# Differential attention: each head's two sample steps placed among its prompt steps, with the weight splitting on them

## The chip, the cores and the metric

The kernel runs on one core of a Trainium2 chip. The metric is the device time of one launch in microseconds. Work is shared by five engines, each with its own in-order queue: TensorE (PE, matrix products and transposes), VectorE (DVE), ScalarE (ACT), GpSimd (POOL) and SyncE (SP); here the last two only start transfers in the stage that is changed. Engines wait for each other on semaphores.

## The reference

One layer of a hybrid encoder, for a prompt of 1024 tokens and a sample of 256, with shared weights. Its differential attention, 4 heads with two maps of depth 64 each and values of width 128:

```
s = einsum('qd,kd->qk', q_c, k_c) * DA_DK ** -0.5 - slope[h] * |pos_q - pos_k|     # c = 0, 1
p_c = softmax(s)
attn = p_0 - lam * p_1
o = attn @ v                                                  # swept over blocks of 128 queries
o_da = head_rms(o, g_da) * (1.0 - lam_init)
mix = concatenate([o_hg, o_da]);  x = x + mix @ w_out         # w_out: 1024 x 1024
```

The prompt and the sample attend only to their own tokens. Before it comes the input projection and the other group of heads (hgrn), behind it the output projection, a cross attention and a mixture of 32 experts.

## The kernel before

The program is a sequence of stages with a barrier between them: `front`, `hgrn`, `diff_attention`, `mix_out`, `project`, `cross_and_experts`. Matrix products are made from operands split into a rounded high part and a low part (three products for one). So a weight must be split before use: ACT rounds it, DVE subtracts.

`diff_attention` works in steps, one for a block of 128 queries (number t) of one head (h): 4 heads with 8 blocks of the prompt, then 4 heads with 2 blocks of the sample, 40 in all. A prompt step has 1024 keys, a sample step 256. The parts of step n and the lines where they stand:

- `scores` (PE, L1309): both score maps, into `score_ps`, which exists once; waits until DVE has read the scores of step n - 1.
- `find_least` (DVE, L1225): adds the distance bias, writes `score` and its least value, for both maps. The trace shows it as CUSTOM_DVE_ANT_0 with a short read of the accumulator behind it.
- `exps` (ACT, L1270): the two exponentials with their sums.
- `attention` (DVE, L1233, L1235, L1238): reciprocal, share, and the difference of the two maps.
- `transposes` (PE, L1319), `copy_attention` (ACT, L1278 and the small L1279), `output` (PE, L1331).
- `head_rstd` (ACT, L1286, L1288, L1290) and `head_norm` (DVE, L1246), after which POOL stores the tile (L1202).

Each engine runs the same outer loop, and in iteration `at` it does its parts of several steps: a part with lead k does step `at + k`. The leads and the order in the iteration are

```
skewed((2, attention), (0, head_norm), (4, find_least), (0, ride))    # DVE
skewed((3, exps), (1, head_rstd), (2, copy_attention), (0, ride))     # ACT
skewed((4, scores), (1, output), (2, transposes))                     # PE
```

`ride` is the weight split: during this stage `w_out` is split in eight pieces of 128 rows (`WeightSplit`). SP loads a piece (L174) into one of two buffers, ACT rounds it (L179, `w_w_high<-da_split_raw`) at the end of its iteration, and DVE subtracts (L184, `w_w_low<-da_split_raw,w_w_high`) at the end of its own, after a wait for ACT's rounding. The table `riders` says in which iterations.

Of the kernel before, what the change touches and what calls it, by code (L numbers as in the profile page):

```python
# [37 lines left out]
P = 128  # L38
D = 1024
KC = D // P  # L40
SEQ_P, SEQ_S, N_MEM = 1024, 256, 256
# [4 lines left out]
HEADS = 4  # L46
# [1087 lines left out]
def diff_attention(nc, tag, dq_t, dk_t, dv_rows, g_da, lam, ident, eps, mix_out, split):  # L1134
# [3 lines left out]

    slopes = [2.0 ** (-8.0 * (h + 1) / HEADS) for h in range(HEADS)]
    width = 2 * SEQ_P - P  # L1140
    steps = [(first, seq, h, t) for first, seq in ((0, SEQ_P), (SEQ_P, SEQ_S)) for h in range(HEADS)
             for t in range(seq // P)]
    N = len(steps)
    riders = {N - KC + r: r for r in range(KC)}
    with Mem(nc, tag) as m:
        keys = m.sb("keys", [P, HEADS, T])
        query = m.sb("query", [P, HEADS, T])
# [26 lines left out]
        def skewed(*parts):  # L1174
            for at in range(-max(lead for lead, _ in parts), N):
                for lead, part in parts:
                    if 0 <= at + lead < N:
                        part(at + lead)

        with nc.Block() as block:  # L1180
            @block.sync
            def _(sp):
                for h in range(HEADS):
                    rows = slice(h * P, (h + 1) * P)
                    sp.dma_start(query[:, h], dq_t[rows, :]).then_inc(qk_in[h], 16)
                    sp.dma_start(keys[:, h], dk_t[rows, :]).then_inc(qk_in[h], 16)
                    if h == 0:
                        sp.dma_start(v[:], dv_rows.rearrange("(t p) c -> p t c", p=P)).then_inc(v_in, 16)
                        with nc.allow_non_contiguous_dma(reason="one row for all partitions"):
                            sp.dma_start(gain[:], g_da.rearrange("(a n) -> a n", a=1).to_broadcast([P, P])  # L1190
                                         ).then_inc(gain_in, 16)
                for r in range(KC):
                    rider.load(sp, r // 2, r % 2)
# [12 lines left out]
            @block.vector  # L1206
            def _(dve):
                rider.start(dve)
                dve.tensor_scalar(minus_lam[:], lam[:], -1.0, None, ALU.mult)
                dve.wait_ge(where_done, 1)  # L1210
                dve.scalar_tensor_tensor(where, where, -1.0, where, ALU.mult, ALU.max).then_inc(distance_done, 1)
                dve.wait_ge(gain_in, 16)
                dve.tensor_scalar(gain[:], gain[:], 1.0 - LAM_INIT, None, ALU.mult)
                dve.drain()

                def find_least(n):
                    first, seq, h, t = steps[n]
                    u, col = n % 2, SEQ_P - P - t * P
                    dve.wait_ge(scores_ready, n + 1)
                    if n < HEADS * SEQ_P // P:  # L1220
                        dve.wait_ge(bias_done, h + 1)
                    if n >= 2:
                        dve.wait_ge(prob_done, n - 1)
                    for c in range(2):
                        done = dve.tensor_tensor_reduce(out=score[:, u, c, 0:seq], in0=score_ps[:, c, 0:seq],  # L1225
                                                        in1=bias[:, h, col:col + seq], scale=1.0, scalar=3.0e38,
                                                        op0=ALU.add, op1=ALU.min, accum_out=least[:, u, c:c + 1])
                    done.then_inc(score_read, 1)

                def attention(n):  # L1230
                    u, seq = n % 2, steps[n][1]
                    dve.wait_ge(prob_done, n + 1)
                    dve.reciprocal(share[:, u:u + 1], total[:, n % 4, 1:2])  # L1233
                    dve.drain()
                    dve.scalar_tensor_tensor(share[:, u:u + 1], total[:, n % 4, 0:1], minus_lam[:, 0:1], share[:, u:u + 1],  # L1235
                                             ALU.mult, ALU.mult)
                    dve.drain()
                    dve.scalar_tensor_tensor(prob[:, u, 0, 0:seq], prob[:, u, 1, 0:seq], share[:, u:u + 1],  # L1238
                                             prob[:, u, 0, 0:seq], ALU.mult, ALU.add).then_inc(attn_done, 1)

                def head_norm(n):
                    u = n % 2
                    dve.wait_ge(rstd_done, n + 1)
                    if n >= 2:
                        dve.wait_ge(stored[u], 16 * (n // 2))
                    dve.scalar_tensor_tensor(o[:, u], o_ps[:, u, 0:P], rstd[:, u:u + 1], gain[:], ALU.mult,  # L1246
                                             ALU.mult).then_inc(o_done, 1)

                def ride(n):
                    if n in riders:  # L1250
                        rider.subtract(dve, riders[n] // 2, riders[n] % 2)

                skewed((2, attention), (0, head_norm), (4, find_least), (0, ride))

            @block.scalar
# [1135 lines left out]
def encoder(nc, x_prompt, x_sample, mem_prompt, mem_sample, g_mix, w_in, hg_lb, g_hg, lam_q1, lam_k1, lam_q2,  # L2391
# [16 lines left out]
    with Mem(nc, "kept") as kept:  # L2408
# [17 lines left out]
        with Mem(nc, "w") as m:  # L2426
            w_at = m.next_address()
            w_high, w_low = m.sb("w_high", [P, KC, D], F32R), m.sb("w_low", [P, KC, D], F32R)
            diff_attention(nc, "da", dq_t, dk_t, dv_rows, g_da[0], lam, ident, eps, mix, (w_out[0], w_high, w_low))
            with Mem(nc, "cq") as m2:  # L2430
                high, low = m2.sb("high", [P, KC, T], F32R), m2.sb("low", [P, KC, T], F32R)
                mix_out(nc, "mix_out", o_fwd, o_bwd, g_rows, mix, x_rows, g_hg[0], w_high, w_low, ident, eps, x1,
                        g_ca[0], high, low)
                project(nc, "proj_q", w_cq[0], D, high, low, TOKEN_GROUPS, q_t, split=(w_co[0], w_high, w_low))
            cross_and_experts(nc, "cross", q_t, kv_t, x1, w_high, w_low, w_at, ident, eps, x2, g_ffn[0], w_rg[0],
                              b_rg[0], w_re[0], b_re[0], h3, w_gate[0].rearrange("e k n -> (e k) n"),
                              w_up[0].rearrange("e k n -> (e k) n"), w_down[0].rearrange("e k n -> (e k) n"), y_rows,
                              g_final, [(y_prompt[0], NT_P), (y_sample[0], NT - NT_P)])
# [28 lines left out]
```

## Time and profile before

| | |
|---|---|
| median of 3 runs | 2228.51 us (2226.96 to 2229.07) |
| the profiled execution | 2223.16 us, of which the span from first to last instruction is 2221.7 us |
| busy share of the span | PE 89%, DVE 62%, ACT 52%, POOL 12% |
| differential attention | from some 735 to 952 us of the span |
| its prompt steps | a step every 4.77 us |
| weight split in it | 8 pieces; ACT 1047 ns and DVE 1225 ns each |
| mean granted PE clock | 0.942 of 2.4 GHz |

Times of a row are microseconds from the start of the span; PEclk is the granted share of 2.4 GHz, so 0.50 is 1.2 GHz. The profile's own chain of what ended last covers only the late stages; for this stage the timeline tells who waits for whom.

### The profile page before, as it was taken

The page shows a single profiled execution, that of the slowest core. Times are in us where ns is not written, and L with a number is a line of the kernel's source. Part 1 is how long each engine was busy: PE and PEld are TensorE (multiplying, and loading weights), DVE is VectorE, ACT ScalarE, POOL GpSimd, SP SyncE. Part 2 cuts the span into 40 slices and gives each one's busy share as a digit, 9 for nine tenths or more (in the row PEclk, how much of TensorE's full clock was granted, in tenths as well). Part 3 has the DMA queues.
Part 4 walks back from the last instruction along what each step waited for, and adds up shares of the span by engine and source line. Part 5 has one row for each costly group of instructions (what it writes and reads, how often), then busy time and mean ns, then how long its engine had stood idle before and what let it go on. Part 6 is the DMA issues. An engine that isn't in the chain of part 4 may idle for free. (4 is left out here: it accounts for less than half of the span.)

```text
span 2221.7 us, 31173 instructions
## 1 busy us (share of the span) xinstructions
PE 1977.8 (89%) x11108; PEld 1639.3 (74%) x11108; DVE 1375.1 (62%) x1841; ACT 1149.1 (52%) x1587; POOL 265.4 (12%) x304
## 2 busy tenths in 40 slices
PE   6999999969999699749989499996999999999990
PEld 5888888857888477438778388885888888888870
DVE  4222231029998488646511035546999999999986
ACT  4334432116665488713222133222888888888873
POOL 0000000020000011100000000000122223232210
PEclk9999999989999899769989799996999999999995
DMA  5223422135553400144233423134899999999987
GB/s 170 102 93 136 144 97 105 47 114 168 164 176 106 179 15 15 63 149 161 95 109 113 149 86 114 61 149 158 324 382 383 383 378 383 377 380 391 378 319 317
DMA packets 162983, 423.97 MB, mean 191 GB/s; under 512 B 18880, under 2 KB 84544, under 8 KB 136768
## 3 DMA queue, kind: packets, MB, share of 16 engines
q1 hardware_dynamic: 137424, 342.37, 43.1%
q0 software_dynamic: 25456, 80.24, 9.4%
q8 instruction: 63, 1.03, 0.2%
q14 instruction: 40, 0.33, 0.0%
HBM read 354.92 MB, written 82.31 MB: 197 GB/s over the span
## 5 line engine op out<-in xcount | busy, mean ns | idle before, releaser
L113 PE MATMUL cross_ot_ps<-w_w_high,cross_o_high 128*128 128x512 f32 x544 | 220.5, 405 | 3.1 <-DVE cross_o_low L2126 2.4
L115 PE MATMUL cross_ot_ps<-w_w_high,cross_o_low 128*128 128x512 f32 x544 | 213.8, 393 | 0.0
L113 PE MATMUL front_acc<-in_high,front_w_high 128*128 128x512 f32 (+1 forms) x480 | 170.3, 355 | 0.0
L114 PE MATMUL front_acc<-in_low,front_w_high 128*128 128x512 f32 (+1 forms) x480 | 170.0, 354 | 0.0
L115 PE MATMUL front_acc<-in_high,front_w_low 128*128 128x512 f32 (+1 forms) x480 | 169.8, 354 | 0.0
L2093 DVE TENSOR_TENSOR cross_low_up<-cross_raw_up,w_w_high 128x2048 fp32r<-128x2048 f32 x68 | 152.8, 2288 | 12.0 <-ACT w_w_high L1904 12.0
L2093 DVE TENSOR_TENSOR cross_low_down<-cross_raw_down,w_w_low 128x2048 fp32r<-128x2048 f32 x68 | 152.7, 2287 | 1.7 <-ACT w_w_low L1904 1.7
L2093 DVE TENSOR_TENSOR w_w_low<-cross_raw_gate,w_w_high 128x2048 fp32r<-128x2048 f32 x68 | 152.2, 2279 | 0.0
L1904 ACT ACTIVATE w_w_high<-cross_raw_up 128x2048 fp32r<-128x2048 f32 x68 | 126.2, 1907 | 0.0
L1904 ACT ACTIVATE w_w_low<-cross_raw_down 128x2048 fp32r<-128x2048 f32 x68 | 126.2, 1907 | 0.0
L1904 ACT ACTIVATE w_w_high<-cross_raw_gate 128x2048 fp32r<-128x2048 f32 x68 | 126.1, 1902 | 0.0
L113 PEld LDWEIGHTS cross_ot_ps<-w_w_high,cross_o_high 128*128 128x128 f32 x544 | 103.2, 190 | 30.1 <-DVE w_w_low L2093 7.2
L115 PEld LDWEIGHTS cross_ot_ps<-w_w_high,cross_o_low 128*128 128x128 f32 x544 | 103.0, 189 | 22.2
L113 PE MATMUL cross_out_ps<-w_w_low,cross_ht 128*128 128x512 f32 x272 | 109.5, 403 | 5.5 <-DVE cross_low_down L2093 5.5
L114 PE MATMUL cross_ot_ps<-w_w_low,cross_o_high 128*128 128x512 f32 x272 | 107.6, 395 | 0.0
L115 PE MATMUL cross_out_ps<-w_w_low,cross_ht 128*128 128x512 f32 x272 | 107.0, 393 | 0.0
L114 PE MATMUL cross_out_ps<-cross_low_down,cross_ht 128*128 128x512 f32 x272 | 106.8, 393 | 0.0
L114 PE MATMUL cross_ot_ps<-cross_low_up,cross_o_high 128*128 128x512 f32 x272 | 106.0, 390 | 0.0
L113 PE MATMUL front_acc<-front_w_high,in_high 128*128 128x512 f32 x240 | 95.2, 397 | 6.0 <-DVE front_w_low L565 6.0
L113 PEld LDWEIGHTS front_acc<-in_high,front_w_high 128*128 128x128 f32 x480 | 90.8, 189 | 12.9
L114 PEld LDWEIGHTS front_acc<-in_low,front_w_high 128*128 128x128 f32 x480 | 90.8, 189 | 12.6
L115 PEld LDWEIGHTS front_acc<-in_high,front_w_low 128*128 128x128 f32 x480 | 90.7, 189 | 12.6
(361 smaller groups left out, 4889.3 us busy)
## 6 DMA issues: line engine op xcount, KB each, us to landing
cross_raw_gate<-in_w_gate_dram SPq DMA_DIRECT2D x68, 1024.0 KB, 7.0
cross_raw_down<-in_w_down_dram SPq DMA_DIRECT2D x68, 1024.0 KB, 7.9
cross_raw_up<-in_w_up_dram SPq DMA_DIRECT2D x68, 1024.0 KB, 9.4
front_raw<-in_w_in_dram SPq DMA_DIRECT2D x32, 512.0 KB, 4.4
hgrn_raw<-in_w_ckv_dram SPq DMA_DIRECT2D x16, 512.0 KB, 6.7
cross_y_kept<-y_rows SPq DMA_DIRECT2D x16, 512.0 KB, 9.4
k_t<-front_staged POOLq DMA_DIRECT2D x8, 640.0 KB, 3.3
lf_t<-front_staged_lf POOLq DMA_DIRECT2D x8, 640.0 KB, 4.6
```

Of the source, the lines that this page charges most:

```text
L113: pe.matmul(out, lhs[0], rhs[0], start=first, stop=False)
L114: pe.matmul(out, lhs[0], rhs[1], start=False, stop=False)
L115: return pe.matmul(out, lhs[1], rhs[0], start=False, stop=last)
L1904: act.activation(w_high[s][:, cols], raw[s][:, cols], ACT.Copy).then_inc(w_high_done[s], 1)
L2093: dve.tensor_tensor(w_low[s][:, cols], raw[s][:, cols], w_high[s][:, cols].bitcast(F32), ALU.subtract).then_inc(w_low_done[s], 1)
```

## The change

The order of the steps is changed. In each head, the two sample steps are put among the eight prompt steps, at places 2 and 7 of ten, so that a sample step is every fifth step (n = 2, 7, 12, ..., 37). The eight pieces of the weight split, which rode on the last eight steps, ride on the sample steps again, which are now spread over the stage. DVE's wait for the bias is made in every step. Sizes, leads, buffers and the number of instructions of each kind are the same; names of lines shift by one (DVE's L1225 is L1226 after).

```diff
-    steps = [(first, seq, h, t) for first, seq in ((0, SEQ_P), (SEQ_P, SEQ_S)) for h in range(HEADS)
-             for t in range(seq // P)]
+    order = [(0, t) for t in range(SEQ_P // P)]
+    for t in range(SEQ_S // P):
+        order.insert(2 + 5 * t, (SEQ_P, t))
+    steps = [(first, SEQ_S if first else SEQ_P, h, t) for h in range(HEADS) for first, t in order]
     N = len(steps)
-    riders = {N - KC + r: r for r in range(KC)}
+    riders = {n: r for r, n in enumerate(n for n in range(N) if steps[n][0])}
...
                     dve.wait_ge(scores_ready, n + 1)
-                    if n < HEADS * SEQ_P // P:
-                        dve.wait_ge(bias_done, h + 1)
+                    dve.wait_ge(bias_done, h + 1)
```

On DVE, at the end of iteration 2 and through iteration 3, early in the stage (`da_` are this stage's tiles, `w_w_high` and `w_w_low` the parts of the weight). Before:

```order
L1225 ISA da_least 128x1
L1233 RECIPROCAL da_share<-da_total 128x1
L1235 SCALAR_TENSOR_TENSOR da_share<-da_total,da_minus_lam,da_share 128x1
L1238 SCALAR_TENSOR_TENSOR da_prob<-da_prob,da_share 128x1024
L1246 SCALAR_TENSOR_TENSOR da_o<-da_o_ps,da_rstd,da_gain 128x128
L1225 ISA da_score,da_least<-da_score_ps,da_bias 128x1024
L1225 ISA da_least 128x1
```

And now:

```order
L1226 ISA da_least 128x1
L184 TENSOR_TENSOR w_w_low<-da_split_raw,w_w_high 128x1024
L1234 RECIPROCAL da_share<-da_total 128x1
L1236 SCALAR_TENSOR_TENSOR da_share<-da_total,da_minus_lam,da_share 128x1
L1239 SCALAR_TENSOR_TENSOR da_prob<-da_prob,da_share 128x1024
L1247 SCALAR_TENSOR_TENSOR da_o<-da_o_ps,da_rstd,da_gain 128x128
L1226 ISA da_score,da_least<-da_score_ps,da_bias 128x256
L1226 ISA da_least 128x1
```

The subtraction of the weight stands between one step's find_least and the attention of a prompt step (128x1024), and the find_least behind that attention is a sample step's (128x256). The same pattern returns every five steps; in all of them but the last it is a prompt step's attention that stands behind the subtraction.

On ACT, at the same iterations (`da_attn_t` is the copy of the transposed attention). Before:

```order
L1278 ACTIVATE da_attn_t<-da_attn_ps 128x1024
L1279 ACTIVATE da_eps_t<-da_total 128x1
L1270 ACTIVATE da_prob,da_total<-da_score,da_least 128x1024 x2
L1286 ACTIVATE da_sq,da_ss<-da_o_ps 128x128
L1288 ACTIVATE da_rstd<-da_ss,da_eps_t 128x1
L1290 ACTIVATE da_rstd<-da_rstd 128x1
```

And now:

```order
L1279 ACTIVATE da_attn_t<-da_attn_ps 128x1024
L1280 ACTIVATE da_eps_t<-da_total 128x1
L179 ACTIVATE w_w_high<-da_split_raw 128x1024
L1271 ACTIVATE da_prob,da_total<-da_score,da_least 128x1024 x2
L1287 ACTIVATE da_sq,da_ss<-da_o_ps 128x128
L1289 ACTIVATE da_rstd<-da_ss,da_eps_t 128x1
```

The rounding of the weight stands behind the copy of a prompt step's transposed attention and ahead of the exponentials of another prompt step.

## Rows read from the trace of the kernel before

**Rows 1.** Busy time by stretch: PE, PEld, DVE, ACT, POOL, PEclk, DMA share, GB/s.
```profile
800.00:850.00 50.00, 50.00 (x338) 35.39 (x338) 44.31 (x85) 42.97 (x106) 5.41 (x10) 1.00 0.04 14
...
935.00:950.00 15.00, 3.83 (x12) 2.44 (x12) 7.15 (x12) 6.62 (x17) 2.16 (x4) 0.50 0.36 122
```

**Rows 2.** Timeline, one prompt step: start, us, engine, line, operation, [idle before <-releaser].
```profile
846.18 2.05 PE L1331 MATMUL da_o_ps<-da_v,da_attn_t 128*128 128x128 f32 x16
...
846.30 1.23 DVE L1225 CUSTOM_DVE_ANT_0 da_score<-da_score_ps,da_bias 128x1024 f32<-128x1024 f32 x1 [0.40 <-PE da_score_ps L1309]
...
848.07 1.04 PE L1319 MATMUL da_attn_ps<-kept_ident,da_prob 128*128 128x128 f32 x8
...
848.27 0.28 ACT L1286 ACTIVATE da_sq<-da_o_ps 128x128 f32<-128x128 f32 x1 [0.50 <-PE da_o_ps L1331]
...
848.59 0.16 DVE L1233 RECIPROCAL da_share<-da_total 128x1 f32<-128x1 f32 x1
...
849.03 1.99 PE L1309 MATMUL da_score_ps<-da_keys,da_query 64*128 64x512 f32 x8
...
849.18 1.01 ACT L1278 ACTIVATE da_attn_t<-da_attn_ps 128x1024 f32<-128x1024 f32 x1
...
850.17 1.14 ACT L1270 ACTIVATE da_prob<-da_score,da_least 128x1024 f32<-128x1024 f32 x1
850.32 0.34 DVE L1246 SCALAR_TENSOR_TENSOR da_o<-da_o_ps,da_rstd,da_gain 128x128 f32<-128x128 f32 x1
...
850.95 1.27 PE L1331 MATMUL da_o_ps<-da_v,da_attn_t 128*128 128x128 f32 x9
850.96 0.54 POOL L1202 DMA_DIRECT2D mix<-da_o  x1 [4.23 <-DVE da_o L1246]
851.07 1.22 DVE L1225 CUSTOM_DVE_ANT_0 da_score<-da_score_ps,da_bias 128x1024 f32<-128x1024 f32 x1 [0.41 <-PE da_score_ps L1309]
```

**Rows 3.** Timeline, a sample step with the first split.
```profile
916.61 0.41 DVE L1225 CUSTOM_DVE_ANT_0 da_score<-da_score_ps,da_bias 128x256 f32<-128x256 f32 x1
...
916.95 0.42 DVE L1225 CUSTOM_DVE_ANT_0 da_score<-da_score_ps,da_bias 128x256 f32<-128x256 f32 x1
...
918.76 1.05 ACT L179 ACTIVATE w_w_high<-da_split_raw 128x1024 fp32r<-128x1024 f32 x1
...
919.91 1.23 DVE L184 TENSOR_TENSOR w_w_low<-da_split_raw,w_w_high 128x1024 fp32r<-128x1024 f32 x1 [2.54 <-ACT w_w_high L179]
...
921.05 0.16 DVE L1233 RECIPROCAL da_share<-da_total 128x1 f32<-128x1 f32 x1
```

**Rows 4.** Timeline, the stage's first steps.
```profile
749.71 1.23 DVE L1225 CUSTOM_DVE_ANT_0 da_score<-da_score_ps,da_bias 128x1024 f32<-128x1024 f32 x1 [0.20 <-issue]
...
752.23 3.79 PE L1309 MATMUL da_score_ps<-da_keys,da_query 64*128 64x512 f32 x8 [7.69 <-DVE da_least L1225]
...
756.05 1.23 DVE L1225 CUSTOM_DVE_ANT_0 da_score<-da_score_ps,da_bias 128x1024 f32<-128x1024 f32 x1 [3.97 <-PE da_score_ps L1309]
...
760.60 1.23 DVE L1225 CUSTOM_DVE_ANT_0 da_score<-da_score_ps,da_bias 128x1024 f32<-128x1024 f32 x1 [0.43 <-PE da_score_ps L1309]
```

**Rows 5.** The tile da_split_raw: idle time before its instructions, us and times.
```profile
  ACT w_w_high L179: 13.7, 8
```

**Rows 6.** Timeline, the end of the stage.
```profile
948.15 1.23 DVE L184 TENSOR_TENSOR w_w_low<-da_split_raw,w_w_high 128x1024 fp32r<-128x1024 f32 x1 [2.25 <-ACT w_w_high L179]
952.47 1.28 ACT L1405 ACT_TABLE_LOAD   x1 [4.42 <-PEq L91]
```

**Rows 7.** The tile da_o: time of its stores from issue to landing.
```profile
DMA to landing us min/median/max: 1.9/1.9/3.2
```

**Rows 8.** Busy time by stretch in the hgrn stage, columns as in rows 1.
```profile
495.00:500.00 5.00, 3.11 (x14) 2.20 (x13) 5.00 (x6) 1.52 (x2) 2.42 (x3) 1.00 1.15 302
500.00:505.00 5.00, 5.00 (x16) 3.96 (x15) 4.76 (x12) 4.93 (x10) 0.57 (x1) 0.66 1.15 307
...
605.00:610.00 5.00, 3.00 (x19) 2.40 (x18) 4.92 (x8) 4.13 (x9) 0.54 (x1) 1.00 0.44 126
```

## The prediction

> **What bounds the kernel now.** The change is inside one stage, the differential attention. It starts near 735 us of the span and ends where the next stage's first ScalarE instruction stands, at 952.47 [rows 6]. I read three views in turn: the busy times by stretch (does one engine fill the stage?), the timeline of one step (what waits for what), and the timeline where the weight split already runs.
>
> By stretch [rows 1] the 32 prompt steps keep TensorE (PE) busy all the time, 50.00 of 50 us at full clock, with VectorE (DVE) at 44.31 and ScalarE (ACT) at 42.97. The last 15 us have PE at 3.83 of 15, at the clock 0.50. That is where the sample steps and the weight split are now, and it invites the change. The three engines are however close to each other in the prompt steps, so extra work there is not free.
>
> The timeline of one step [rows 2] shows how close. Each step comes 4.77 us after the last (DVE's L1225 at 846.30 and at 851.07), because PE's three parts fill it: output at 846.18, transposes at 848.07 (1.89 later), scores at 849.03 (0.96 later), output again at 850.95 (1.92 later); 1.89 + 0.96 + 1.92 = 4.77. DVE works 4.37 of it and waits 0.40 for the scores. A second loop lies just below: there is one score tile in PSUM, so PE's scores (1.99) and DVE's find_least (2.29, from 846.30 to 848.59, and 0.09 for its last read of the accumulator, 2.38) take turns, 4.37 plus two hand-overs, and the start of the stage shows that loop alone at 4.55 (756.05 to 760.60) [rows 4].
>
> **The change, part by part.** No instruction is added or removed. The 32 large and 8 small steps and the 8 weight splits are the same; what moves is which part stands beside which. With sample steps at 2, 7, 12, ..., 37 and leads of 0 to 4, every iteration holds exactly one part of a sample step. Four of five lighten an engine; in the fifth, lead 0, the sample step gives only its head_norm and brings a weight split.
>
> *The wait that the split brings.* In the iteration's order, DVE subtracts after its find_least, and ACT rounds after its copy of the attention tile. On ACT that point comes late: it follows PE's transposes. In the step of [rows 2], DVE is through with find_least and goes on with the next step at 848.59; ACT is through with the copy, and at its next exponential, at 850.17. With a split there, ACT rounds from 850.17 for 1.05 [rows 3], DVE sees it 0.10 later, at 851.32, and so has stood for 851.32 - 848.59 = 2.73 us. The queue is in order: behind the subtraction stand the next step's attention, and behind that PE's transposes. The trace already has this wait where steps are small: 2.54 at the first split [rows 3], 13.7 over eight splits [rows 5]. So the wait is seen, only smaller, since there ACT's part is shorter.
>
> *Interval of a sample step.* From one find_least's end to the next: wait 2.73, subtraction 1.14 (919.91 to the next DVE instruction at 921.05) [rows 3], attention 1.73 (848.59 to 850.32), head_norm 0.27 (its 0.34 overlapped by the next start) [rows 2], and the small find_least, two times 0.34 or 0.69 (916.61 to 916.95 is one) [rows 3]. Sum 6.55 with rounding. Without the split it would be 2.69.
>
> *Interval of a prompt step.* Where PE's output or transposes are the small ones, the score loop sets it, 4.54; where PE has three large parts it stays 4.77. Following the queues from the start, of the 30 intervals after the first, 21 take 4.54 and 9 take 4.77.
>
> *Sum of the stage, clock kept.* find_least of step 0 starts at 749.71 [rows 4] in both. First interval 6.34 (749.71 to 756.05, cold PE); step 2's, whose turn comes before any split, attention 1.73 and the small find_least 0.69, 2.42; 9 x 4.77 = 42.93; 21 x 4.54 = 95.34; 7 x 6.55 = 45.85. Together 192.88, so step 39's find_least starts at 942.59. That step is a prompt step now, and its drain is long. In series, from [rows 2]: find_least 2.38, two exponentials of 1.14 and a read 2.37, attention with its last write 1.81, transposes 1.04, copy 1.01, output 2.05, the norm's ACT steps 1.0 (848.27 to the copy at 849.18 and a last write), head_norm 0.34, and seven hand-overs of 0.05, 0.35: 12.35. Two queue waits come on top, 0.8 for the exponentials behind step 36's and 37's ACT parts and 1.85 for the transposes behind output of step 38: 15.0, to 957.6. Then 0.3 to the store's issue (850.32 + 0.34 to 850.96) [rows 2], 1.9 to its landing [rows 7], and the 3.1 that now lie between the last work's end (948.15 + 1.23) and the next stage at 952.47 [rows 6]: 962.9. That is **+10.4 us**. The last split's subtraction (step 37) ends before the last head_norm and adds nothing; its loads are issued a whole group ahead, and land in some 3 us.
>
> *The clock.* Now PE works without a gap through the prompt steps and is granted 1.00 [rows 1]. After the change it waits at each split. In the times of [rows 2], with a split there: the small scores run from 849.03 to about 849.6; output waits for the copy's end, 850.25, a gap of 0.66, and leaves PE free at 852.14; DVE's attention starts at 851.32 + 1.14 = 852.46 and ends at 854.27, so the transposes start at 854.33, a gap of 2.20. That is some 2.7 busy of 5.3 us, 51%. The trace has cases on both sides: after 3.11 busy of 5 us, with one gap, PE was granted a mean of 0.66 in the next 5 us, so 3.4 us of them at 1.2 GHz though it was busy throughout; after 3.00 of 5 in another stretch it stayed at 1.00 [rows 8]. What a fall costs: cold scores take 3.79 [rows 4] against 1.99 [rows 2], and they are in the loop that sets the pace, so 1.8 us each. The bounds are 0 and 7 falls before the drain, 0 and 12.6 us; the stretches lie on either side of mine, so I take three, 5.4. In the drain PE is mostly idle, and its transposes and output of 1.04 and 2.05 would take up to 2.9 more when cold; I take 2.2. Sum of the clock: 7.6, and the forecast **10.4 + 7.6 = +18 us**.
>
> The Trainium skill, TensorE: Matmul & The Clock Gate, section "HAM oscillation — how this bites in real kernels", says that a PE that waits between tiles for its operands loses its clock and starts the next tile cold, in its example at every tile. The trace bears out the mechanism but not the "every" [rows 8]. By that rule all seven places before the drain would fall.
>
> **The rivals.**
> *The clock stays at 2.4 GHz.* Only the wait is paid: +10.4, 2238.9. For it: the stretch with 3.00 of 5 us that kept 1.00 [rows 8]. Against it: each of my places has both of its gaps in a row.
> *The clock falls at every split.* 10.4 + 12.6 + 2.9 = +25.9, 2254.4. For it, the fall after 3.11 of 5 us; and every place of this kernel has more idle time than that stretch had. The rule of the Trainium skill's TensorE page, above, would give this.
> *Faster: ACT's rounding isn't late.* If ACT had rounded by the time DVE comes, each of seven intervals would be 2.73 shorter and PE would have no gap to lose its clock in: 10.4 - 19.1 = -8.7, 2219.8. It decides when the wait is under (19.1 - 10.4 - 4.5)/7 = 0.6 us. For it: the engines' own work allows it, since PE needs 4 x 4.77 + 1.6 = 20.7 us for five steps, below the 24.9 forecast. Against: ACT's copy can't precede PE's transposes, and 850.17 stands beside 848.59 [rows 2].
> *No change.* A wait of about 1.3 us in place of 2.73, by parts of ACT that slip forward after the small exponentials, gives 10.4 - 7 x 1.4 = +0.6, 2229. The first split's 2.54 with small parts [rows 3] speaks against it.
>
> **How the numbers follow.** The profiled execution took 2223.16 us (span 2221.7 and 1.5 around it); with +18 it gives 2241.2. The median of the runs shown is 5.35 above it, 2228.51; the forecast for the median is 2246.5. Chances: two to five falls of the clock (+14 to +22) 0.53, no fall 0.19, every one 0.14, faster 0.07, no change 0.07. The range of 8 in 10 reaches from +6.5 (the unfallen case with a wait half a microsecond shorter) to +28 (every fall, and two microseconds more in the drain): 2235 to 2256.5. A difference of 0.2%, 4.5 us, is about what this kernel's runs can tell from none. Faster 0.07, same 0.07, slower 0.86.
>
> **What would show it.** In the changed kernel's timeline: DVE's L184 with about 2.7 us idle before it, put down to ACT's L179, eight times and some 20 us in all (now 13.7); find_least intervals of 4.5 to 4.8 between prompt steps and 6.5 across a split; PE idle for 2.2 us before transposes after each split; a granted clock below 1.00 in some of these places; the next stage's table load at 963 with the clock kept, near 970 with the falls. It is wrong if DVE's wait there is under 1 us, if the prompt intervals stay at 4.77 or rise, or if the clock falls and stays down over several steps, which would cost tens of microseconds.

## The result

| | median, us | lowest to highest | against before |
|---|---|---|---|
| before | 2227.74 | 2226.72 to 2229.07 (4 runs) | |
| changed | 2248.81 | 2246.06 to 2252.29 (4 runs) | 1.0096, 95% interval 1.0081 to 1.0111 |

The changed kernel is 21 us slower; 2246.5 was forecast, within 2235 to 2256.5. In the profiles the differential attention takes 240.3 us, from its first table load at 733.8 to the next stage's at 974.1, and took 217.3 before (735.2 to 952.5), so 23.0 more. The stages behind it take 1272.6 in this profile and 1269.2 in that of before; in the twelve experiments, which don't touch them, they take 1271.6 to 1275.1, in both orders of the steps, so nothing puts the 3.4 down to the change.

The busy time by stretch of the changed kernel, columns as in [rows 1]:

```profile
765.00:800.00 35.00, 30.67 (x205) 21.61 (x204) 28.10 (x58) 27.12 (x72) 3.80 (x7) 1.00 0.07 27
800.00:850.00 50.00, 42.30 (x261) 28.70 (x259) 36.74 (x79) 36.00 (x95) 4.84 (x9) 0.93 0.10 35
850.00:900.00 50.00, 42.24 (x264) 28.69 (x265) 37.98 (x81) 37.94 (x100) 5.39 (x10) 0.97 0.10 35
900.00:950.00 50.00, 42.08 (x270) 29.21 (x270) 38.99 (x82) 37.35 (x99) 4.85 (x9) 0.97 0.07 23
```

Where PE was busy for 50.00 of 50 us it is now at 42, and DVE and ACT have fallen too, to 37 to 39 and 36 to 38 from 44.31 and 42.97. No engine is the bound of this stage any more: they wait for each other. The granted clock is below 1.00 in each of the three long stretches.

The timeline of the changed kernel at a split, which answers to [rows 2]:

```profile
803.44 2.05 PE L1332 MATMUL da_o_ps<-da_v,da_attn_t 128*128 128x128 f32 x16
803.55 1.23 DVE L1226 CUSTOM_DVE_ANT_0 da_score<-da_score_ps,da_bias 128x1024 f32<-128x1024 f32 x1 [0.18 <-PE da_score_ps L1310]
...
805.33 1.04 PE L1320 MATMUL da_attn_ps<-kept_ident,da_prob 128*128 128x128 f32 x8
...
805.84 0.08 DVE L1226 DVE_READ_ACCUMULATOR2_ANT da_least<- 128x1 f32 x1
...
806.30 0.70 PE L1310 MATMUL da_score_ps<-da_keys,da_query 64*128 64x256 f32 x4
...
806.44 1.01 ACT L1279 ACTIVATE da_attn_t<-da_attn_ps 128x1024 f32<-128x1024 f32 x1
...
807.44 1.04 ACT L179 ACTIVATE w_w_high<-da_split_raw 128x1024 fp32r<-128x1024 f32 x1
...
807.50 2.05 PE L1332 MATMUL da_o_ps<-da_v,da_attn_t 128*128 128x128 f32 x16 [0.50 <-ACT da_attn_t L1279]
...
808.58 1.23 DVE L184 TENSOR_TENSOR w_w_low<-da_split_raw,w_w_high 128x1024 fp32r<-128x1024 f32 x1 [2.66 <-ACT w_w_high L179]
...
811.60 1.19 PE L1320 MATMUL da_attn_ps<-kept_ident,da_prob 128*128 128x128 f32 x8 [2.04 <-DVE da_prob L1239]
...
811.72 0.42 DVE L1226 CUSTOM_DVE_ANT_0 da_score<-da_score_ps,da_bias 128x256 f32<-128x256 f32 x1
```

Read it down DVE's column. find_least is over at 805.92 (805.84 and 0.08). The next DVE work starts at 808.58 and is the subtraction; the 2.66 us before it are put down to ACT's L179. ACT starts that rounding at 807.44, as it is through with the copy of 806.44, and the copy waited for PE's transposes of 805.33. Behind the subtraction stands the attention, so PE, through with its output at 809.55, idles 2.04 us before its transposes.

In the whole stage the wait is, from the tile da_split_raw of the changed kernel (before: 13.7, [rows 5]):

```profile
  ACT w_w_high L179: 25.0, 8
```

And the clock behind that gap, in the busy times:

```profile
812.00:817.00 5.00, 5.00 (x22) 2.46 (x21) 3.03 (x9) 2.09 (x6) 1.08 (x2) 0.66 0.19 75
```

A mean of 0.66 over 5 us means 3.4 us at 1.2 GHz (0.50) and the rest at 2.4, with PE busy throughout; the scores there take 3.54 in place of 1.99. Such a fall of 3.4 us comes behind four of the seven splits ahead of the drain.

### The profile page after: what moved, and what is told of

It reads as the page before. It is cut to its first block and busy times, and to the rows that moved or that the text cites. A ratio compares the mean times of both kernels' runs of the same rounds, so it can differ in the third digit from the quotient of the medians.

```text
span 2246.7 us, 31173 instructions
## 1 busy us (share of the span) xinstructions
PE 1986.8 (88%) x11108; PEld 1644.7 (73%) x11108; DVE 1374.7 (61%) x1841; ACT 1147.8 (51%) x1587; POOL 264.7 (12%) x304
## 5 line engine op out<-in xcount | busy, mean ns | idle before, releaser
L113 PE MATMUL cross_ot_ps<-w_w_high,cross_o_high 128*128 128x512 f32 x544 | 220.3, 405 | 3.1 <-DVE cross_o_low L2127 2.4
L2094 DVE TENSOR_TENSOR cross_low_up<-cross_raw_up,w_w_high 128x2048 fp32r<-128x2048 f32 x68 | 152.8, 2288 | 12.1 <-ACT w_w_high L1905 12.1
L1310 PE MATMUL da_score_ps<-da_keys,da_query 64*128 64x512 f32 (+1 forms) x288 | 80.4, 677 | 29.7 <-DVE da_least L1226 20.4
L114 PEld LDWEIGHTS front_acc<-in_low,front_w_high 128*128 128x128 f32 x480 | 90.9, 189 | 12.6
L115 PEld LDWEIGHTS front_acc<-in_high,front_w_low 128*128 128x128 f32 x480 | 90.8, 189 | 12.6
```

Source lines behind the costliest of these rows:

```text
L113: pe.matmul(out, lhs[0], rhs[0], start=first, stop=False)
L114: pe.matmul(out, lhs[0], rhs[1], start=False, stop=False)
L115: return pe.matmul(out, lhs[1], rhs[0], start=False, stop=last)
L1310: last = pe.matmul(score_ps[:, c, at:at + size], query[half, h, first + t * P:first + (t + 1) * P], keys[half, h, first + at:first + at + ...
L2094: dve.tensor_tensor(w_low[s][:, cols], raw[s][:, cols], w_high[s][:, cols].bitcast(F32), ALU.subtract).then_inc(w_low_done[s], 1)
```

## The experiments

All edits are to `diff_attention`. Times are medians; the ratio is to the kernel before, measured beside each on the same chip. There its median was 2225.83 for the first four kernels of the table, 2227.43 for dve_later, act_earlier, keep_busy and spread_act_earlier, and 2226.25 for the other four; so kernels of different groups are compared by their ratios (the changed kernel has 1.0096). "Stage" is the time between the two table loads in the run's profile, 217.3 before and 240.3 in the changed kernel. The wait in the last column is that of the splits inside the stage's loop.

| kernel | time, us | ratio, 95% interval | stage | DVE's wait for ACT's rounding |
|---|---|---|---|---|
| order_only | 2239.92 | 1.0068, 1.0051 to 1.0085 | 232.3 | 18.1 |
| spread_only | 2243.14 | 1.0076, 1.0060 to 1.0093 | 231.7 | 21.5 |
| behind_before | 2230.30 | 1.0022, 1.0011 to 1.0032 | 220.3 | |
| behind_after | 2240.95 | 1.0074, 1.0057 to 1.0091 | 231.7 | |
| dve_later | 2227.60 | 1.0002, 0.9993 to 1.0012 | 220.3 | 2.2 |
| act_earlier | 2225.59 | 0.9991, 0.9981 to 1.0000 | 217.8 | 0.8 |
| keep_busy | 2259.11 | 1.0147, 1.0129 to 1.0166 | 250.8 | 37.1 |
| keep_busy_gap | 2243.05 | 1.0079, 1.0063 to 1.0096 | 233.8 | 25.0 |
| spread_act_earlier | 2220.77 | 0.9975, 0.9965 to 0.9984 | 212.7 | 3.0 |
| before_act_earlier | 2219.69 | 0.9972, 0.9961 to 0.9983 | 210.5 | 5.2 |
| last_places | 2223.31 | 0.9986, 0.9977 to 0.9996 | 215.2 | 0.7 |
| spread_both | 2219.46 | 0.9972, 0.9963 to 0.9982 | 211.3 | 0 |

### One half of the change at a time

`order_only`, the changed order with the splits on the last eight steps:

```diff
-    riders = {n: r for r, n in enumerate(n for n in range(N) if steps[n][0])}
+    riders = {N - KC + r: r for r in range(KC)}
```

> The changed order of the steps, but the weight splits on the last eight steps as before. Theory (an in-order wait at each split, and a score loop of 4.54 us that keeps the interleaved steps from giving back what a small step saves): following the queues, the stage ends some 9 to 12 us later than before, so about 2238, with DVE's L184 idle before it 16 us in all. Rival (only splitting among large steps costs; the interleaved order by itself hides the sample steps): the time is at or below that of before, 2215 to 2228.

`spread_only`, the order of before with the splits spread (against the kernel before):

```diff
-    riders = {N - KC + r: r for r in range(KC)}
+    riders = {2 + 5 * r: r for r in range(KC)}
```

> The order of the steps as before, but the splits on steps 2, 7, ..., 37, all of them but one among large steps. Theory: DVE waits 2.7 us at each of the seven among large steps, about 20 to 22 us in all, and PE, which waits in turn, loses its clock at about half of them; the small steps at the end lose their splits and become shorter. Following the queues +9 with the clock kept and about +15 with it lost, 2237 to 2243. Rival (the split's cost comes from its standing beside sample steps): about as before, 2224 to 2232.

Both halves cost by themselves, 15 us in the stage (232.3) and 14.4 (231.7); both rivals fall. The theory was somewhat short in both: 9 to 12 us were expected of `order_only` and at most 15 of `spread_only`, and the ratios give 15 and 17. The splits cost because of the large parts around them, whatever the order of the steps, and the order costs even with the splits where they were, or nearly: the last eight steps now have six large ones among them, and 18.1 us of waits.

### The order without any split in it

To take the splits out of the comparison, they are put behind the last step, in the kernel before and in the changed one:

```diff
-    riders = ...
+    riders = {}
...
                 skewed((2, attention), (0, head_norm), (4, find_least), (0, ride))
+                for r in range(KC):
+                    rider.subtract(dve, r // 2, r % 2)
...
                 skewed((3, exps), (1, head_rstd), (2, copy_attention), (0, ride))
+                for r in range(KC):
+                    rider.round(act, r // 2, r % 2)
```

> The order of before, and all eight splits behind the last step. They add one after the other some 20 us behind the last step in this kernel and in the next, and take away what they cost inside. Expected +4 to +8 against before, 2232 to 2236. It is the base for the next run.

> The changed order, and all eight splits behind the last step: against the run before it only the order of the steps differs, and no split stands inside. Theory (the order by itself costs, since the score loop of 4.54 us bounds most prompt steps and the stage ends on two large steps): 8 to 11 us slower than with the order of before, 2241 to 2246, with PE's clock kept inside the stage. Rival (the order by itself gains, all the loss is from the waits at the splits, 7 x 2.7): 5 to 10 us faster than with the order of before.

The stage is 11.4 us longer with the changed order, 231.7 against 220.3, and the time 10.7 us, 2240.95 against 2230.30. The difference is where the theory had it, and the rival's gain doesn't come. The 11.4 have two parts. From the first find_least to the last it takes 174.1 with the order of before and 180.2 with the changed one, 6.1 more; and from the last find_least to the end of the last head_norm, the drain, it takes 9.4 and 15.3, 5.8 more, because a large step is now the last. Why the small steps among large ones aren't hidden is seen in DVE's timeline of `behind_after`, here find_least alone (the second of each pair of maps left out):

```profile
791.78 1.23 DVE L1226 CUSTOM_DVE_ANT_0 da_score<-da_score_ps,da_bias 128x1024 f32<-128x1024 f32 x1 [1.20 <-PE da_score_ps L1314]
...
796.33 1.23 DVE L1226 CUSTOM_DVE_ANT_0 da_score<-da_score_ps,da_bias 128x1024 f32<-128x1024 f32 x1 [0.18 <-PE da_score_ps L1314]
...
800.88 1.23 DVE L1226 CUSTOM_DVE_ANT_0 da_score<-da_score_ps,da_bias 128x1024 f32<-128x1024 f32 x1 [0.18 <-PE da_score_ps L1314]
...
805.17 0.41 DVE L1226 CUSTOM_DVE_ANT_0 da_score<-da_score_ps,da_bias 128x256 f32<-128x256 f32 x1
...
809.72 1.23 DVE L1226 CUSTOM_DVE_ANT_0 da_score<-da_score_ps,da_bias 128x1024 f32<-128x1024 f32 x1 [0.47 <-PE da_score_ps L1314]
...
814.49 1.22 DVE L1226 CUSTOM_DVE_ANT_0 da_score<-da_score_ps,da_bias 128x1024 f32<-128x1024 f32 x1 [1.21 <-PE da_score_ps L1314]
```

Five steps take 814.49 - 791.78 = 22.71 us. Four prompt steps took 4 x 4.77 = 19.1, so the small one costs 3.6. In `behind_before` the eight small steps at the end take 24.5 from one find_least to the next (898.88 to 923.37), 3.1 each: the first ones more, while parts of large steps are still under way, and the last ones 2.23:

```profile
921.14 0.41 DVE L1225 CUSTOM_DVE_ANT_0 da_score<-da_score_ps,da_bias 128x256 f32<-128x256 f32 x1
...
923.37 0.41 DVE L1225 CUSTOM_DVE_ANT_0 da_score<-da_score_ps,da_bias 128x256 f32<-128x256 f32 x1
...
932.46 0.35 DVE L1246 SCALAR_TENSOR_TENSOR da_o<-da_o_ps,da_rstd,da_gain 128x128 f32<-128x128 f32 x1 [2.24 <-ACT da_rstd L1292]
```

The same end of the loop in `behind_after`, on two large steps:

```profile
928.05 1.23 DVE L1226 CUSTOM_DVE_ANT_0 da_score<-da_score_ps,da_bias 128x1024 f32<-128x1024 f32 x1 [1.20 <-PE da_score_ps L1314]
...
942.95 0.35 DVE L1247 SCALAR_TENSOR_TENSOR da_o<-da_o_ps,da_rstd,da_gain 128x128 f32<-128x128 f32 x1 [3.71 <-ACT da_rstd L1293]
```

Eight times the difference (3.63 - 3.06) is 4.6 of the 6.1; the rest lies in the stage's first steps. The parts of a small step fall into five iterations, one for each lead. In each of them the other leads' parts are those of large steps, and so another engine, or the one score tile that PE and DVE hand to each other (4.55 from 791.78 to 796.33 and again to 800.88), still has its full length. PE, at 92% in this kernel and at 100% in the prompt steps of before, shows it:

```profile
800.00:850.00 50.00, 45.91 (x308) 32.34 (x305) 41.63 (x89) 40.12 (x109) 5.95 (x11) 1.00 0.04 16
```

### The wait at the split

`dve_later` lets DVE subtract one iteration later (and `skewed` run one iteration longer):

```diff
-            for at in range(-max(lead for lead, _ in parts), N):
+            for at in range(-max(lead for lead, _ in parts), N + 1):
...
-                skewed((2, attention), (0, head_norm), (4, find_least), (0, ride))
+                skewed((2, attention), (0, head_norm), (4, find_least), (-1, ride))
```

> The changed kernel, but DVE subtracts one iteration later than ACT rounds (lead -1 in place of 0), at the end of its iteration. No instruction is added or removed. Theory (the in-order wait of DVE for ACT's rounding, and the clock that PE loses behind it, are the larger part of the loss): the 25 us of idle time before L184 fall under 3, no fall of the clock at the splits, and the stage ends some 20 us earlier than in the changed kernel, at about 2228, within 3 us of before. Rival (the subtraction's own 1.2 us in DVE's queue, or the order of the steps, is what costs): 2244 or more.

`act_earlier` moves the rounding to where ACT waits for PE's output:

```diff
-                skewed((3, exps), (1, head_rstd), (2, copy_attention), (0, ride))
+                skewed((3, exps), (0, ride), (1, head_rstd), (2, copy_attention))
```

> The changed kernel, but ACT rounds the weight behind the exponentials, where it waits for PE's output anyway, and not behind the copy. DVE's place is unchanged. Theory: DVE's wait goes from 25 us to about 1 and the time is 1 to 2 us below the run with the later subtraction, 2226 to 2229. Rival (rounding ahead of the norm and the copy makes these late, and PE and DVE wait for them): 2240 or more.

Either edit alone, of one or two lines and with no instruction more or less, takes the whole loss away: the ratios are 1.0002 and 0.9991 against 1.0096. `dve_later` came where the theory had it, `act_earlier` 0.4 us below its range of 2226 to 2229. The timeline of `act_earlier` at a split:

```profile
802.39 1.04 ACT L179 ACTIVATE w_w_high<-da_split_raw 128x1024 fp32r<-128x1024 f32 x1
...
804.13 1.22 DVE L184 TENSOR_TENSOR w_w_low<-da_split_raw,w_w_high 128x1024 fp32r<-128x1024 f32 x1
...
807.25 0.41 DVE L1226 CUSTOM_DVE_ANT_0 da_score<-da_score_ps,da_bias 128x256 f32<-128x256 f32 x1
...
810.67 1.23 DVE L1226 CUSTOM_DVE_ANT_0 da_score<-da_score_ps,da_bias 128x1024 f32<-128x1024 f32 x1 [0.48 <-PE da_score_ps L1310]
```

The rounding is over at 803.43, and the subtraction follows DVE's own work with no idle time. It costs nothing there: five steps take 22.71 (784.54 to 807.25 from one small find_least to the next), as in `behind_after`, which has no split among them. DVE comes early behind the small find_least of each group and would wait, and the subtraction fills that wait. The stage is 217.8.

### The clock

`keep_busy` was to keep PE busy in its gap:

```diff
+                def keep_busy(n):
+                    if n in riders and n < N - 3:
+                        pe.wait_ge(o_done, n + 1)
+                        for _ in range(16):
+                            pe.transpose(o_ps[:, n % 2, P:2 * P], ident[:], ident[:])
+
-                skewed((4, scores), (1, output), (2, transposes))
+                skewed((4, scores), (1, output), (0, keep_busy), (2, transposes))
```

> The changed kernel with its waits, and 16 transposes of the identity into unused columns of o_ps (1.8 us, nobody reads them) in PE's gap of 2.0 to 2.2 us at seven of the eight splits. They do nothing for the result. Theory (the falls of the clock cost 1.8 us each, on top of the wait): no fall of the clock at the four splits where it fell, DVE's waits unchanged at 2.66, and the time 6 to 8 us below the changed kernel, 2241 to 2243. Rival (a fall costs nothing since PE has slack there): as the changed kernel, 2247 to 2250.

This missed, and by my placing: the gap is one iteration later. Here the 1.8 us stand ahead of the transposes on which ACT's copy waits, and behind the copy comes the rounding. So the run measures something else, PE's work ahead of the copy. In its timeline the wait has grown from 2.66 to 4.39:

```profile
815.47 1.23 DVE L184 TENSOR_TENSOR w_w_low<-da_split_raw,w_w_high 128x1024 fp32r<-128x1024 f32 x1 [4.39 <-ACT w_w_high L179]
```

Seven times 1.73 is 12.1, and the waits went from 25.0 to 37.1. The stage grew by 10.5. The clock still fell behind three of the seven splits, one fewer than in the changed kernel. So the run can't tell whether a fall costs anything. `keep_busy_gap` has them in the right place:

```diff
+                def keep_busy(n):
+                    if n in riders and n < N - 3:
+                        for _ in range(16):
+                            pe.transpose(attn_ps[:, 0:P], ident[:], ident[:])
+
-                skewed((4, scores), (1, output), (2, transposes))
+                skewed((4, scores), (1, output), (-1, keep_busy), (2, transposes))
```

> The changed kernel with its waits, and 16 transposes of the identity (1.8 us, nobody reads them) one iteration later than in keep_busy: behind PE's output of the iteration that follows a split, in the gap of 2.0 to 2.2 us that PE has there, ahead of no work that anybody waits for. They go into attn_ps, which is free then. Theory (a fall of the clock costs about 1.8 us, and PE's gap is what brings it): DVE's waits at 2.66 as in the changed kernel, no fall at the splits, and a time 6 to 8 us below the changed kernel, 2241 to 2243. Rival (a fall costs nothing, PE has slack behind it): 2247 to 2250.

PE's timeline and busy times in `keep_busy_gap`:

```profile
811.64 1.91 PE L1339 MATMUL da_attn_ps<-kept_ident 128*128 128x128 f32 x16
813.84 1.09 PE L1320 MATMUL da_attn_ps<-kept_ident,da_prob 128*128 128x128 f32 x8 [0.30 <-DVE da_prob L1239]
814.88 1.99 PE L1310 MATMUL da_score_ps<-da_keys,da_query 64*128 64x512 f32 x8
...
800.00:850.00 50.00, 45.57 (x310) 32.88 (x308) 39.57 (x83) 39.16 (x104) 5.40 (x10) 1.00 0.10 35
850.00:900.00 50.00, 45.58 (x310) 32.88 (x308) 39.68 (x83) 39.16 (x104) 5.40 (x10) 1.00 0.10 35
900.00:950.00 50.00, 44.79 (x307) 32.40 (x303) 39.67 (x83) 39.27 (x103) 5.41 (x10) 1.00 0.07 25
```

The clock stays at 1.00, the waits are the same 25.0, and the stage is 6.5 us shorter than the changed kernel's: four falls at 1.6 each, a little under the 1.8 of theory. The times alone don't show it: the ratios, 1.0079 and 1.0096, are 4 us apart and their intervals overlap. But the changed kernel's own timeline has the same price. From one small find_least to the next it takes 24.99 where the clock was kept (786.73 to 811.72), and 26.61 over the fall shown above, from 811.72 to

```profile
838.33 0.41 DVE L1226 CUSTOM_DVE_ANT_0 da_score<-da_score_ps,da_bias 128x256 f32<-128x256 f32 x1
```

The two other groups with a fall between two such find_leasts take 26.62 and 26.68. In `keep_busy_gap` all six take 24.98 or 24.99. The rival, no price, falls.

### Towards a faster kernel

`spread_act_earlier` has the edits of `spread_only` and `act_earlier`, `before_act_earlier` only the latter in the kernel before, `spread_both` those of `spread_only`, `act_earlier` and `dve_later`. `last_places` is `act_earlier` with

```diff
-        order.insert(2 + 5 * t, (SEQ_P, t))
+        order.insert(4 + 5 * t, (SEQ_P, t))
```

> The order of the steps as before, the splits on steps 2, 7, ..., 37, and ACT's rounding behind the exponentials. Theory (a split among large steps is almost free once DVE doesn't wait for it, since PE bounds these steps, and the small steps at the end become shorter without it): 7 to 9 us faster than before, 2219 to 2221. Rival (DVE's 1.14 us for a subtraction among large steps lengthens each of these steps in full, 8 x 1.14, and eats the gain): 2226 to 2230.

> The kernel before, order and places of the splits untouched, but ACT's rounding behind the exponentials and not behind the copy. Theory (the wait of DVE for ACT's rounding costs there too, 13.7 us among small steps at half the clock): 5 to 7 us faster than before, 2220 to 2222, that is nearly all that the same edit with the spread splits gave. Rival (it was the spreading that gained): 2225 to 2228.

> As act_earlier, but the sample steps at places 4 and 9 of ten and not at 2 and 7, so that the stage starts on four large steps and ends on a small one. Theory (a part of what the interleaved order costs by itself is the clock at the start, 6.8 us at 1.2 GHz from step 2 on, and the drain behind two large steps): 2 to 4 us faster than act_earlier, 2222 to 2224. Rival (the loop of 4.54 us is all of it, the places don't matter): as act_earlier, within 1 us.

> As spread_act_earlier, and DVE subtracts one iteration later as well, so that it never waits for ACT. Theory (3.0 us of waits are left there, in part on the path): 1 to 2 us faster than spread_act_earlier, 2219. Rival (what is left of the waits lies beside other waits): the same within 1 us, 2220 to 2221.

`before_act_earlier` is the plainest of the fast ones: 0.9972, 0.28% faster than the kernel before, by one moved part. The wait of 13.7 us among the small steps is 5.2. With the spread splits on top the ratio is 0.9975 or 0.9972, with intervals that overlap, so spreading brings nothing that can be measured, and the rival that credited it falls. Between `spread_both` and `spread_act_earlier` the runs don't decide. The stage of `last_places` is 2.6 us shorter than that of `act_earlier`, as theory had it, but only one of theory's two reasons holds. Its drain behind the last find_least, now a small one, takes 12.6 in place of 16.3. Its start gains nothing: PE is at 1.2 GHz until some 763, and step 3's find_least starts 17.3 us behind step 0's, where `act_earlier` takes 16.2. The intervals of the two ratios, 0.9986 and 0.9991, overlap, so of its time a gain isn't shown.

One pair answers what the order costs once DVE no longer waits at the splits: `act_earlier` and `spread_act_earlier` differ only in the order of the steps (with the wait for the bias that goes with it), and were measured side by side. The changed order takes 2225.59 and the old one 2220.77, 4.8 us less, and the stages are 217.8 and 212.7. From the first find_least to the last the changed order even takes 1.1 us less (180.0 and 181.1); its drain takes 5.9 more (16.3 and 10.4). What the order still costs is its end on large steps.

## Why the prediction was right

The time came nearer than the sum did: the stage is 23.0 us longer where 18 was forecast, the time 21. That the time is within 2.3 us of the forecast is in part luck, since the changed kernel's own runs lie 6 us apart.

*The wait.* 2.73 us was forecast from [rows 2], 2.66 is measured, seven times (18.5 us); the eighth, in the drain, is 6.5 and the sum of 25.0 is above the 20 forecast, but that one is off the path, as forecast. `act_earlier` and `dve_later` show that it decides.

*The intervals.* A group of five steps was put at 3 x 4.54 + 4.77 + 6.55 = 24.94. In the changed kernel, with the clock kept, the small find_least stands at 786.73 and again at 811.72, 24.99 apart:

```profile
786.73 0.41 DVE L1226 CUSTOM_DVE_ANT_0 da_score<-da_score_ps,da_bias 128x256 f32<-128x256 f32 x1
...
789.67 1.22 DVE L1226 CUSTOM_DVE_ANT_0 da_score<-da_score_ps,da_bias 128x1024 f32<-128x1024 f32 x1 [0.18 <-PE da_score_ps L1310]
```

*The clock.* Three falls before the drain and 7.6 us in all were forecast. There were four behind splits, at 1.6 each, and one that had no term in the sum: after the small scores of step 2, PE runs at 1.2 GHz for 6.8 us from 757.8 on, so the large scores of step 3 start at the lower clock at 760.80 and take 3.79:

```profile
757.25 0.70 PE L1310 MATMUL da_score_ps<-da_keys,da_query 64*128 64x256 f32 x4 [2.56 <-DVE da_least L1226]
...
760.80 3.79 PE L1310 MATMUL da_score_ps<-da_keys,da_query 64*128 64x512 f32 x8
764.64 1.23 DVE L1226 CUSTOM_DVE_ANT_0 da_score<-da_score_ps,da_bias 128x1024 f32<-128x1024 f32 x1 [3.27 <-PE da_score_ps L1310]
```

Step 3's find_least starts 16.1 us behind step 0's (748.52), and 13.5 was in the sum: 2.6 more. Of these the longer scores are 1.8. The kernel before takes 15.4, with a large step in step 2's place, so the small one, which was to save 1.9 here, cost 0.7. That it is the cause of the lower clock isn't shown: in `last_places`, whose first four steps are large, PE is at 1.2 GHz for longer still.

*The end.* Drain with the cold part: 17.2 forecast, 16.6 measured (950.94 to the last head_norm's end at 967.55). From there to the next stage I had 5.3, by the distance of 3.1 from the last subtraction; it is 6.5:

```profile
967.20 0.35 DVE L1247 SCALAR_TENSOR_TENSOR da_o<-da_o_ps,da_rstd,da_gain 128x128 f32<-128x128 f32 x1 [0.55 <-ACT da_rstd L1291]
967.85 0.54 POOL L1204 DMA_DIRECT2D mix<-da_o  x1 [0.36 <-DVE da_o L1247]
974.07 1.28 ACT L1406 ACT_TABLE_LOAD   x1 [6.90 <-PEq L91]
```

The last store is issued 6.2 us ahead of the next stage, and before the change 6.3 (946.19 to 952.47), though there a split ended in between; in `act_earlier` and `dve_later` it is 6.2 too. So it is the store, and not the last split, that the stage's end is counted from where no work follows.

*The sum.* The next stage was put at 970.5 (962.9 and 7.6) and came at 974.1. The first find_least stood 1.2 earlier than in the sum, the first steps took 2.6 more, the falls 1.1 more (6.5 in place of 5.4), the other intervals 0.4 more, the drain 0.6 less and the end 1.2 more. Most of the missing 3.6 us lies at the two ends of the stage.

*What was wrong* is in the rival "ACT's rounding isn't late". It took 7 x 2.73 off and came to -8.7 us. `act_earlier` is that case, and it is at -1.8 us (0.9991); its stage is 0.5 longer than before. The prediction took the small step's interval as 2.69 without a wait or a split, and the next ones as unchanged. The 2.69 is right: in `behind_after` find_least ends at 803.25 (800.88 + 2.37) and, small, at 805.93. But the next large one then ends at 812.09 (809.72 + 2.37), 6.16 later and not 4.54, since DVE, early behind the small find_least, waits 1.23 for ACT's exponentials and 0.47 for PE's scores:

```profile
805.51 0.42 DVE L1226 CUSTOM_DVE_ANT_0 da_score<-da_score_ps,da_bias 128x256 f32<-128x256 f32 x1
...
807.16 0.16 DVE L1234 RECIPROCAL da_share<-da_total 128x1 f32<-128x1 f32 x1 [1.23 <-ACT da_prob L1273]
```

Five steps take 22.71 without any split and 24.99 with one: the split's wait and its subtraction, 3.8 us of DVE's time, cost 2.3, because they cover the 1.7 that DVE would wait anyway. So of the rival's 2.73 at each split only 2.3 could be had, and the first steps, the drain and the end are longer in `act_earlier` as well than in the sum. And the interleaved order costs 11.4 with no split at all; the prediction has this only inside its sum, as a loop of 4.54 and a long drain. The waits were not the only obstacle to a gain: without them the change stands where the kernel before stood, and 4.8 us behind `spread_act_earlier`.

Two readings of the prediction were off without changing its sum. "Exactly one part of a sample step" in every iteration should be the parts of one lead: with lead 2 these are attention, copy and transposes, on three engines. And with gaps of 0.66 and 2.20 in 5.3 us PE is busy for 2.4 us and not 2.7; the trace has gaps of 0.50 and 2.04 there.

## What to carry to other kernels

When work in two halves (round here, subtract there) rides along in in-order queues, look at the moment at which each engine comes to it in its own iteration. Here that difference of 2.7 us, read from one steady step, cost 2.3 for each of seven splits and led to the falls of the clock; moving one half by one place took it away, and the same move gained 0.28% in the old kernel.

Small steps put among large ones gave no gain here. When parts are staggered by leads, a small step shortens a few parts in each iteration, and another engine or a shared buffer still sets the pace. And the last step matters: with a large one at the end the drain was 5.8 to 5.9 us longer, with and without splits in the loop.

A gap on PE can be charged twice, once as waiting and once as a slower clock behind it: four of seven gaps were, at 1.6 us each.

## What the runs showed of the hardware

The granted clock fell behind four of seven gaps that were alike in length, 2.04 us of waiting each, and each time for 3.4 us at 1.2 GHz though PE was busy in them; what set the four apart from the three no run here shows. With transposes of the identity in the gap it stayed at 2.4 GHz in all seven (granted 1.00 from 785 to 950). The Trainium skill, TensorE: Matmul & The Clock Gate, "Part 4: PE-mode transpose", says that products in transpose mode don't count as busy in the same way. Whether these are in that mode the trace doesn't say; those in the gap did keep the clock up.
